# Modulation rows turned by VectorE instead of TensorE, and a new wait on the weight fetches, in a two-block transformer kernel on one core

## What is computed

```python
def conv_glu(x, w_in, conv_w, conv_b, w_out):            # first block, twice
    gate, val = jnp.split(x @ w_in, 2, axis=-1)
    gate = conv_general_dilated(gate, conv_w, ...) + conv_b
    return (jax.nn.gelu(gate, approximate=False) * val) @ w_out

def ada_params(sc, w, b):                                # second block, per layer
    mod = sc @ w + b                                     # sc: 2 rows, w: 1024 x 6144
    return [t[:, None, :] for t in jnp.split(mod, 6, axis=-1)]
```

## Time and profile before

| | us |
|---|---|
| median of 3 runs (lowest, highest) | 2168.85 (2167.91, 2170.43) |
| the profiled execution's own time | 2168.83 |
| its span, first to last instruction | 2167.1 |
| TensorE busy | 1961.5 (91%) |
| GpSimd busy | 1268.1 (59%) |
| VectorE busy | 1122.0 (52%) |
| ScalarE busy | 1005.2 (46%) |
| loop of `f0`, from 312.8 to 476.6 | 163.8 |
| loop of `f1`, from 966.5 to 1132.2 | 165.7 |

### The profile page before, as it was taken

One profiled execution on the slowest core, in us unless ns is written; L12 is line 12 of the kernel. 1 busy time (PEld: TensorE's weight loads), 2 busy tenths in 40 slices (PEclk: granted clock), 3 DMA queues, 4 the chain that ended last, 5 costly groups with the idle time before them and its releaser, 6 DMA issues.

```text
span 2167.1 us, 34254 instructions
## 1 busy us (share of the span) xinstructions
PE 1961.5 (91%) x13757; PEld 1736.7 (80%) x13757; DVE 1122.0 (52%) x1489; ACT 1005.2 (46%) x1694; POOL 1268.1 (59%) x588
## 2 busy tenths in 40 slices
PE   6889989999899989989999889998879997978997
PEld 6878788888799966868888878876669986947996
DVE  7773247770200074137776565678755632845641
ACT  4454434443344463434544344468734545424542
POOL 9737556669688702646559434400377985415985
PEclk9999999999899999999999999999999998988999
DMA  6325256674455503356675222311234543314543
GB/s 248 139 93 194 98 221 267 269 268 178 158 192 187 185 19 134 120 218 243 264 283 180 79 78 78 117 59 59 78 127 175 188 181 117 136 58 146 191 178 116
DMA packets 48320, 342.29 MB, mean 158 GB/s; under 512 B 5264, under 2 KB 6288, under 8 KB 7248
## 3 DMA queue, kind: packets, MB, share of 16 engines
q1 hardware_dynamic: 45968, 328.22, 41.4%
q0 software_dynamic: 2240, 12.49, 1.5%
HBM read 339.65 MB, written 1.05 MB: 157 GB/s over the span
## 4 chain that ended last, share of the span: by engine, by line
PE 60%; DVE 21%; ACT 8%; DMA 4%; issue 3%; POOL 3%; DVEq 0%; SPq 0%; ACTq 0%; POOLq 0%
PE bank L1653 12%; PE bank L1599 9%; PE bank L1603 9%; PE bank L1601 9%; DMA ring<-slabs_dram 4%; DVE arena L853 2%; PE bank L1697 2%; POOL w_lo L2079 2%; PE bank L1203 2%; PE bank L1205 2%; PE bank L1206 2%; PE bank L1634 2%; PE bank L1633 2%; PE bank L1631 2%; ACT arena L1057 2%
## 5 line engine op out<-in xcount | busy, mean ns | idle before, releaser
L2079 POOL TENSOR_TENSOR w_lo<-ring,w_hi 128x1024 fp32r<-128x1024 f32 x360 | 880.7, 2469 | 322.7 <-ACT w_hi L2586 322.5
L1599 PE MATMUL bank<-x_hi,w_hi 128*128 128x256 f32 x2176 | 618.7, 284 | 30.5 <-POOL w_lo L2079 16.9
L1603 PE MATMUL bank<-x_lo,w_hi 128*128 128x256 f32 x2176 | 620.8, 285 | 0.0
L2586 ACT ACTIVATE w_hi<-ring 128x1024 fp32r<-128x1024 f32 x448 | 448.7, 1052 | 283.8 <-DMA ring<-slabs_dram 283.8
L1599 PEld LDWEIGHTS bank<-x_hi,w_hi 128*128 128x128 f32 x2176 | 416.6, 191 | 52.4 <-issue 44.8
L1603 PEld LDWEIGHTS bank<-x_lo,w_hi 128*128 128x128 f32 x2176 | 416.0, 191 | 0.0
L1601 PE MATMUL bank<-x_hi,w_lo 128*128 128x256 f32 x1472 | 412.9, 281 | 0.0
L2524 ACT ACTIVATE arena<-bank 128x512 f32<-128x512 f32 (+1 forms) x274 | 142.6, 535 | 354.8 <-PE bank L1603 248.1
L2079 POOL TENSOR_TENSOR w_hi<-ring,w_hi 128x1024 fp32r<-128x1024 f32 x88 | 217.5, 2493 | 137.9 <-ACT w_hi L2586 137.9
L1601 PEld LDWEIGHTS bank<-x_hi,w_lo 128*128 128x128 f32 x1472 | 280.9, 191 | 0.0
L1601 PE MATMUL bank<-x_hi,w_hi 128*128 128x256 f32 x704 | 200.5, 285 | 0.0
(11 more groups left out here) (332 smaller groups left out, 3679.4 us busy)
## 6 DMA issues: line engine op xcount, KB each, us to landing
ring<-slabs_dram SPq DMA_DIRECT2D x312, 1024.0 KB, 4.8
lnrow<-ln_dram POOLq DMA_DIRECT2D x6, 1024.0 KB, 5.1
xt<-xT_dram SPq DMA_DIRECT2D x1, 1024.0 KB, 5.8
xt<-memT_dram POOLq DMA_DIRECT2D x1, 1024.0 KB, 13.5
x<-x_dram POOLq DMA_DIRECT2D x1, 1024.0 KB, 17.4
arena<-ctx_dram POOLq DMA_DIRECT2D x1, 1024.0 KB, 8.8
lnrow<-ln_dram POOLq DMA_DIRECT2D x2, 512.0 KB, 4.6
res<-x POOLq DMA_DIRECT2D x2, 512.0 KB, 2.9
```

The costliest lines, as they stand in the source:

```text
L1599: ins = pe.matmul(dst, wh[:, k, c], src[0][:, k, :], start=(k == 0), stop=False)
L1603: ins = pe.matmul(dst, wh[:, k, c], src[1][:, k, :], start=False, stop=(k == KC - 1))
L2079: pool.tensor_tensor(dst[:, c], ring[:, s, c], w_hi[:, s, c].bitcast(F32), ALU.subtract).then_inc(S["lo_ready"], 1)
L2586: a.activation(w_hi[:, g % RING, c], ring[:, g % RING, c], ACT.Copy) \
```

## The change

Five things are different. The line numbers behind them are those of the kernel after.

1. `ada_T` and its 48 small products per stage are gone from TensorE's loop. Instead VectorE turns each bank of modulation rows, in blocks of 32 x 32, into `modR` (`turn_ada`, L2274), as the first instruction of its step, and frees the bank itself.
2. ScalarE's `ada_out` no longer reads the bank: it picks the 16 useful values per partition out of `modR` into `modC` (L2667), and it stands behind the GELU of its step instead of ahead of the `raw` copy. It waits for VectorE's turn of the same step.
3. After the loop VectorE turns the last two banks after its own step 21, the second of them only when ScalarE has picked those up to number 22. ScalarE picks 22 and 23 before it rounds the second fo-slab.
4. TensorE puts the columns in place with four products of 32 x 96 (`ada_columns`, L1823) before slab 2 of the fo-stage. VectorE's `modulation` waits for them. `pick` grows from 2 to 32 columns.
5. SyncE waits for GpSimd (`lo_ready`) and not for `slab_begun` before network slabs 5, 7, ... 43 of `f0` and `f1`. It asks that GpSimd has finished the slab that lay in the slot before. The even slabs wait as before, and the queue keeps its order.

```diff
-            def ada_T(j, r):
-                pe.wait_ge(free_of(5 + r % 2), frees(5 + r % 2))
-                for ch in range(2):
-                    at = 2 * (2 * j + ch)
...
-                    ins = pe.matmul(dst, modR[:, r, ch * P:(ch + 1) * P], pick, start=True,
-                                    stop=True)
+            def ada_columns(layer):
+                pe.wait_ge(free_of(4), frees(4))
+                pe.wait_ge(S["ada_kept"], 24 * (layer + 1))
+                kept = modC.rearrange("p u (c q s) -> p q (u c) s", c=2, q=4)
+                for q in range(4):
+                    ins = pe.matmul(bank[4][32 * q:32 * (q + 1), 0:96].rearrange("p (a s) -> p a s", s=2),
+                                    pick, kept[:, q, :, :], start=True, stop=True)
+                fill(ins, 4, "dve")
...
-                rows_split(f"fo{layer}", hook=turn_ctx if layer else None)
+                def between(j):
+                    if j == 2:
+                        ada_columns(layer)
+                    if layer:
+                        turn_ctx(j)
+                rows_split(f"fo{layer}", hook=between)
...
+            for layer in range(2):
+                for n in range(2, FC):
+                    halves_read[FIRST[f"f{layer}"] + 2 * n + 1] = marks[f"lo_f{layer}"] + 2 * (n - 1)
+            for g in range(SLABS):
+                if g in halves_read:
+                    sp.wait_ge(S["lo_ready"], halves_read[g])
+                elif g >= RING:
+                    sp.wait_ge(S["slab_begun"], g - 2)
...
+            def turn_ada(u):
+                b = 5 + u % 2
+                v.wait_ge(full["dve"][b], L.filled(b))
+                v.transpose(modR[:, u % 2, :], bank[b][:, 0:256]).then_inc(free["dve"][b], 1)
+                v.wait_ge(free["dve"][b], L.freed(b))
...
                     for u in range(4):
+                        if conv is not None:
+                            turn_ada(u)
                         gated(i, u, conv)
...
+                if conv is not None:
+                    turn_ada(2)
+                    v.wait_ge(S["ada_kept"], 24 * conv + 22)
+                    turn_ada(3)
...
-                def ada_out(u):
-                    copy_out(5 + u % 2, modR[:, u, :], bank[5 + u % 2][:, 0:256])
+                def ada_out(u, j):
+                    b = 5 + u % 2
+                    a.wait_ge(free["dve"][b], L.up(("turned", b)))
+                    a.activation(modC[:, j, :].rearrange("p (c s) -> p c s", s=2),
+                                 modR[:, u % 2, :].rearrange("p (c s) -> p c s", s=32)[:, :, 0:2],
+                                 ACT.Copy).then_inc(S["ada_kept"], 1)
...
                 def one(i, u):
-                    if conv:
-                        ada_out(u)
-                    else:
+                    if not conv:
...
                     a.activation(act[:, u, :], src, func).then_inc(S["act_ready"], 1)
+                    if conv:
+                        ada_out(u, i * 4 + u)
```

More of the change, by code:

```diff
@@ L246, in build @@
         half16 = small[:, 136:152]
-        pick = small[:, 152:154]
+        pick = small[:, 264:296]
         modA = small[:, 168:184]
@@ L282, in build @@
         goT = tri[:, :, :, :].rearrange("p a b c -> p (a b c)").rearrange("p (a b) -> p a b", a=8)
-        modR = cut(15360, 4, 256)
+        modR = cut(15360, 2, 256)
+        modC = cut(15872, 24, 16)
         raw = cut(11264, 4, 512)
@@ L1503, in build @@
         marks = {}
-        @block.sync
-        def _(sp):
-            sp.dma_start(xT, xT_in).then_inc(S["in_xT"], 16)
-            for g in range(SLABS):
-                if g >= RING:
-                    sp.wait_ge(S["slab_begun"], g - 2)
-                sp.dma_start(ring[:, g % RING, :], slabs[SOURCE[g]]).then_inc(landed[g % RING], 16)
         @block.tensor
@@ L1822, in ada @@
                     begun(ins, k == 0 and last_one)
[L1823 to L1835 removed]
+                fill(ins, b, "dve")
+            def ada_columns(layer):
[6 more added lines that the diff above has]
+                fill(ins, 4, "dve")
             def network(layer):
@@ L1844, in network @@
                 marks[stage] = {q: L.now(("act", q)) for q in range(8)}
+                marks[f"ada{layer}"] = {b: L.now(("dve", b)) for b in (5, 6)}
                 turned = turned_x()
-                pe.wait_ge(free_of(4), frees(4))
                 for b_ in (5, 6):
                     pe.wait_ge(free_of(b_), frees(b_))
-                    last[b_] = "act"
-                per = {("act", q): 2 if q > 4 else 1 for q in (0, 1, 2, 3, 5, 6)}
+                    last[b_] = "dve"
+                per = {("act", q): 1 for q in range(4)} | {("dve", q): 2 for q in (5, 6)}
                 with L.rounds(5, per | {("took", "lo_ready"): 8}) as i:
@@ L1855, in network @@
                         col_T_split(stage, 2 * u + 1, u, waits=turned if u == 0 else None)
-                        ada_T(i * 4 + u, u)
                 for u in range(2):
@@ L2126, in _ @@
                 if k == 4:
+                    marks["lo_f1"] = L.now(("took", "hi_ready"))
                     lo("f1", 1)
@@ L2141, in _ @@
                     lo("xk1", 3)
+                    marks["lo_f0"] = L.now(("took", "hi_ready"))
                     lo("f0", 1)
@@ L2154, in _ @@
             more_pool(pool, L, rstd, ln_rows, lo, los)
+        @block.sync
+        def _(sp):
+            sp.dma_start(xT, xT_in).then_inc(S["in_xT"], 16)
+            halves_read = {}
+            for layer in range(2):
[6 more added lines that the diff above has]
+                    sp.wait_ge(S["slab_begun"], g - 2)
+                sp.dma_start(ring[:, g % RING, :], slabs[SOURCE[g]]).then_inc(landed[g % RING], 16)
         @block.vector
@@ L2322, in network @@
                 per = {k: 4 * n for k, n in one.items()} | {("raw", b): 1 for b in range(4)}
+                if conv is not None:
+                    per |= {(k, b): 2 for k in ("bank", "freed") for b in (5, 6)}
                 with L.rounds(5, per) as i:
                     for u in range(4):
+                        if conv is not None:
+                            turn_ada(u)
                         gated(i, u, conv)
                 for u in range(2):
+                    if conv is not None:
+                        turn_ada(u)
                     gated(5, u, conv)
+                if conv is not None:
+                    turn_ada(2)
+                    v.wait_ge(S["ada_kept"], 24 * conv + 22)
+                    turn_ada(3)
             split_x("dq", by_chunks)
@@ L2380, in _ @@
             v.wait_ge(S["consts"], L.took("consts"))
-            v.tensor_reduce(pick, ident.rearrange("p (q c) -> p c q", q=4)[:, 0:2, :], AX.X,
+            v.tensor_reduce(pick, ident.rearrange("p (q c) -> p c q", q=4), AX.X,
                             ALU.add).then_inc(S["pick_ready"], 1)
@@ L2663, in one @@
                     a.activation(act[:, u, :], src, func).then_inc(S["act_ready"], 1)
+                    if conv:
+                        ada_out(u, i * 4 + u)
                 per = {("bank", b): 1 for b in range(4)} | {("freed", b): 1 for b in range(4)}
                 if conv:
-                    per |= {("took", "pre_ready"): 4} | {(k, b): 2 for k in ("bank", "freed") for b in (5, 6)}
+                    per |= {("took", "pre_ready"): 4, ("turned", 5): 2, ("turned", 6): 2}
                 if conv:
+                    L.n.update({("turned", b): marks[f"ada{layer}"][b] for b in (5, 6)})
                     hi(net, 3)
```

11 lines of the change are left out of this document (2 added, 9 removed).

## The result

The changed kernel takes 2179.35 us, median of 5 runs (2176.82 to 2181.24), beside 2168.21 us for the kernel before on the same chip. The ratio is 1.0042, 95% interval 1.0022 to 1.0061: between 4.8 and 13.2 us slower. The profiled execution took 2178.69 us, its span 2177.0.

What follows compares the result with a forecast made beforehand. VectorE, held while GpSimd subtracts, with ScalarE's GELU in between, was taken as the bound. Terms of 3.75 + 3.5 + 6.0 + 1.7 + 1.2 + 0.9 = 17 us on 2168.83 gave 2186 us, range 2170 to 2204.

Steps and rivals of the forecast that it cites:

- the loops stay at 7.8: Rival for both f-loops: the step pattern keeps drifting and only the ends cost 10 us, 2179 us; chance 15%.
- The bound: In both f-loops, VectorE, held while GpSimd subtracts, with ScalarE's GELU in between, sets the step, 7.94 us in the trace.
- The turn: VectorE's added instruction per step: 0.42 us, not held by GpSimd, hidden behind a standstill except in a round's first step.
- The loops: Both f-loops, first GELU to last `raw` copy: steps of 8.0 us, 3.75 us more in `f0`, 3.5 in `f1`.
- The start of slab 1: Loop ends: the second fo-slab is rounded behind two picks, so TensorE waits 3.0 us for it, twice, 6.0 together.
- The low clock: Fo-stages: a wait may bring one more low-clock stretch, 1.7 us in half the cases; 1.7 us for both.
- Columns and `rstd`: Fo-stages: four column products on TensorE's path, 1.2 us for both, and slab 3 late behind `rstd` in `fo1`, 0.9 us.
- The fetches: SyncE's changed wait in `f0` and `f1`: both slabs are released by one signal as before, so 0 us.
- Paid in full: Rival for both loops: the turn lengthens steps to up to 8.6 us, 11 us more per loop, 2208 us; chance 17%.
- TensorE is released: Rival for both loops: they run at the slab's way, 6.96 us per step, 2142 us; 8%, and 7% for half.

Runs made afterwards that it cites:

- e4: Kernel after, with VectorE's convolution and product reading gate and value from the PSUM bank and ScalarE's raw copy left out in both loops: 2139.07 us, ratio 0.9851.
- e9: e4 with a copy of the raw copy's size, which nothing reads, put back in ScalarE's queue: 2138.23 us, ratio 0.9861 to the kernel before.
- e10: Kernel after, with each of ScalarE's picks of 16 columns done three times, two of them into unused places: 2185.90 us, ratio 1.0087 to the kernel before.
- e2: Kernel after, with every VectorE turn of a modulation product done twice, 48 more instructions: 2184.71 us, ratio 1.0068 to the kernel before.
- e1: Kernel after, with SyncE's network fetches waiting again for the whole slab one ring ahead, not GpSimd's last read: 2178.94 us, ratio 1.0032 to the kernel before.
- e7: Kernel after, with two more unused two-column products on TensorE in each of the 40 steps inside the rounds: 2178.21 us, ratio 1.0036 to the kernel before.
- e3: Kernel after, with ScalarE rounding slab 1 right behind the last GELU of each loop, ahead of two picks: 2171.60 us, ratio 1.0012 to the kernel before.

## Why the prediction came out as it did

The sign and the mechanism held. The predicted 2186 is 7 us too high. The measured 2179 is the very number that I had given for "the loops stay at 7.8", but that rival's reason was a pattern that keeps drifting, and the pattern locked. Term by term, for both stages, in the profiled executions:

- **The bound: right.** VectorE's standstills beside GpSimd set the step; e4, e9 and e10 show it from three sides. One support was misread. The 12.5 us of the earlier trace rows can't lie in the loop of `f0`, since TensorE is idle there for only 163.80 - 156.14 = 7.66 us. In the loop it waits 5 times for that copy, 6.3 us together; the rest is the wait behind the loop, counted for the products and for the weight loads.
- **The turn: right.** Predicted 0.42 us and not held, measured 0.45. The row it rested on was thin: the copy of the earlier trace rows ran beside GpSimd for only 0.16 us, from 1276.81 to 1276.97. The turn is hidden in a steady step (e2) and open in the first step of a round.
- **The loops: right in kind, mis-sized.** Predicted 7.25 us more, measured 1.1. The largest error is the steady step: 8.0 predicted, 7.77 measured. I wrote that the small pick takes the place of the copy, "so GpSimd still starts at about +2.2". The 128x256 copy and the 128x16 pick don't cost ScalarE the same: the pick holds the `raw` copy back by 0.11 us, and GpSimd starts at +2.03. 2.03 + 4.79 + 0.94 is 7.76; I had 7.94 from the earlier trace rows and rounded up. In 28 steady steps that is 6.4 us too much. The start of the loops, put at 1.3 us each, took 2.3, which by luck hides 2.0 of it. The last part, from the GELU of step 18 to R, took 12.8 instead of 13.6, as the 0.8 that I had added for a low clock didn't come: the granted clock there is 1.00.
- **The start of slab 1: right in place, too large.** 3.0 us later in each stage predicted, 1.84 and 1.79 measured. GpSimd had it at R + 10.75 and was through at R + 15.6, where I had R + 16.8: step 21's GELU came at R + 6.8 instead of 7.4, and from there to the rounding it took 2.85 us instead of 3.4.
- **The low clock: right in size, by luck.** 1.7 us predicted for both stages, as an even chance of 1.7 in each. One such stretch came, in `fo0`, where slab 1 takes 1.6 us longer than before. In `fo1` none follows the wait. Its slab 0 has 5.2 us at the lower level where the kernel before had 3.5, but TensorE would have waited for slab 1 anyway. In e1 that stretch came in both stages, the wait in `fo0` was 0.61 us, no low clock followed it, and from R to the addition it took 66.17 us and not 67.75. So this term is a property of the execution. Why the first stretch is longer at one time than at another, no run shows.
- **Columns and `rstd`: right in sum.** 0.38 us for the columns in each stage (0.6 predicted), 1.17 us for slab 3 (0.9 predicted). With the two terms before, these make 7.2 of the 7.8 us at the ends. The last 0.6 us aren't traced.
- **The fetches: right.** 0 predicted. SyncE's 146.9 us in 21 waits are 146.8 in 21, and e1 shows no difference.
- **The rivals.** "Paid in full" fell to e2, "TensorE is released" to the steps and to e7. It comes true when VectorE's reads are moved (e4).

## What to carry to other kernels

- Before moving work to another engine, find which instructions set the period. Here TensorE was busy 95% of the loop before, and what the change took from it became idle time (e7). VectorE and GpSimd, busy 75 and 62%, set the steps, because one of them stands while the other works.
- A new instruction beside a standstill was free here (e2), and one of 0.1 us ahead of the instruction that starts the standstill was paid in every steady step (e10). Ask of each what it delays, not how long it is. For a period that repeats, take it from rows to a hundredth of a us and don't round. A useful count is how many instructions are held in each step.
- Look at the last step too. The slab behind the loop was late because its rounding stood behind small picks that wait for VectorE's last turns; moving it ahead gave back most of the loss (e3).
- When a wait looks shorter in one place than in another, check whether the work before it took longer. The start time against a fixed event (slab 1 at R + 15.6 in both stages) shows the delay, and the wait alone doesn't.

## What the runs showed of the hardware

- VectorE's turn of a 128x256 bank in 32 x 32 blocks took 449 to 452 ns in all 48 cases, with and without GpSimd at work.
- A `scalar_tensor_tensor` with one operand in PSUM and one in SBUF took 0.48 us beside GpSimd's subtraction; with both in SBUF 2.4 us (L2260 in e4, L2257 in the kernel after).
- Three instructions of 16 columns in a row on ScalarE start 0.11 us behind one another, though each is listed with 0.20 (e10).
